# A decoder step on one core: the first pair's tokens gathered before gain and bias, a shifted first ring, and head means in fewer columns

## What is computed

```python
proj = x @ w_in                      # q, k, v of two head groups, 8 heads x 64 each
o_A = block-sparse attention over k, v (all past 256 positions here)
o_B = dilated attention, windows 128/1, 512/4, 2048/16, merged by denominators
o = concat(RMSNorm_head(o_A) * gn_moba, RMSNorm_head(o_B) * gn_win) @ w_out
x = LayerNorm(alpha * x + o)         # ln1_g, ln1_b
top-4 of 32 experts by softmax router; per expert:
  gu = x @ w_gate_up + b; act = clamped SwiGLU(gu); y = act @ w_down + b_down
x = LayerNorm(alpha * x + sum of gate * y)   # ln2_g, ln2_b
```

## Time and profile before

| | |
|---|---|
| median of 3 runs | 1183.83 us (1183.76 to 1184.81) |
| profiled execution, its own time | 1188.98 us |
| its span | 1187.1 us |
| mean granted TensorE clock | 0.986 of full |
| busy: TensorE, VectorE, ScalarE, GpSimd | 1141.0, 297.0, 175.3, 38.4 us |
| HBM read, written | 450.43 MB, 11.93 MB |

### The profile page before, as it was taken

The page is one execution under the profiler, slowest core; times in us unless marked ns, Lnnn a source line. Parts: engine busy times, 40 slices in busy tenths (PEclk is TensorE's granted clock), DMA queues, the critical chain, the costliest instruction groups (busy, mean ns, idle before and its releaser), DMA issues.

```text
span 1187.1 us, 14412 instructions
## 1 busy us (share of the span) xinstructions
PE 1141.0 (96%) x5520; PEld 469.3 (40%) x5521; DVE 297.0 (25%) x702; ACT 175.3 (15%) x381; POOL 38.4 (3%) x71
## 2 busy tenths in 40 slices
PE   8999889999999999999999999999999999999996
PEld 6877654553333333333333333333333333333332
DVE  1453756822021212121211203030303030303113
ACT  1332322211010101010202010101010111111111
POOL 0110111200000000000000000000000000000001
PEclk9999999889999999999999999999999999999998
DMA  9957749758999999999999999999999999999993
GB/s 350 320 195 255 266 176 413 305 199 344 407 427 426 428 428 427 428 428 428 428 428 428 428 428 428 428 427 428 428 428 428 428 428 427 428 428 428 413 422 123
DMA packets 83397, 454.45 MB, mean 383 GB/s; under 512 B 7146, under 2 KB 20098, under 8 KB 36130
## 3 DMA queue, kind: packets, MB, share of 16 engines
q1 hardware_dynamic: 81008, 441.49, 90.2%
q0 software_dynamic: 1728, 10.75, 2.4%
q10 hardware_dynamic: 626, 1.75, 0.4%
HBM read 450.43 MB, written 11.93 MB: 389 GB/s over the span
## 4 chain that ended last, share of the span: by engine, by line
PE 75%; DMA 18%; DVE 4%; ACT 2%; SPq 1%; issue 1%; DVEq 0%
PE bank L1055 23%; PE bank L1097 18%; DMA ring<-in_w_gate_up 16%; PE bank L1031 8%; PE bank L688 6%; PE bank L665 5%; PE bank L1122 3%; PE bank L835 2%; PE bank L691 2%; DMA ring<-in_w_down 2%; PE bank L1206 1%; PE bank L790 1%; PE bank L1138 1%; PE bank L956 1%; SPq L448 1%; ACT actT L1286 1%
## 5 line engine op out<-in xcount | busy, mean ns | idle before, releaser
L1055 PE MATMUL bank<-ring,xg 128*64 128x512 f32 x1904 | 420.6, 598 | 10.6 <-DMA ring<-in_w_gate_up 10.6
L1055 PEld LDWEIGHTS bank<-ring,xg 128*64 128x64 f32 x1904 | 133.6, 137 | 288.9 <-issue 263.6
L1097 PE MATMUL bank<-ring,actT 128*64 128x512 f32 x960 | 215.9, 597 | 3.8 <-ACT actT L1286 3.8
L1888 DVE TENSOR_TENSOR acc<-acc,bank 128x512 f32<-128x512 f32 x60 | 41.2, 687 | 493.6 <-PE bank L1122 493.6
L1097 PEld LDWEIGHTS bank<-ring,actT 128*64 128x64 f32 x960 | 66.6, 137 | 121.5 <-issue 118.7
L1429 ACT ACTIVATE sig<-gate 128x256 f32<-128x256 f32 x64 | 26.7, 417 | 528.0 <-DVE gate L1870 528.0
L1031 PE MATMUL bank<-hx,pick 128*128 128x512 f32 x180 | 90.0, 625 | 0.0
L1870 DVE TENSOR_SCALAR gate<-bank 128x256 f32<-128x256 f32 x64 | 26.9, 420 | 186.7 <-PE bank L1055 166.5
L688 PE MATMUL bank<-xT,wblk 128*128 128x288 f32 x256 | 68.4, 423 | 0.9 <-DVE xT L1517 0.9
L1122 PE MATMUL bank<-ybuf,spread 128*128 128x512 f32 x120 | 58.4, 618 | 0.0
L688 PEld LDWEIGHTS bank<-xT,wblk 128*128 128x128 f32 x256 | 49.4, 198 | 16.4 <-issue 2.4
(11 more groups left out here) (236 smaller groups left out, 724.1 us busy)
## 6 DMA issues: line engine op xcount, KB each, us to landing
ring<-in_w_gate_up SPq DMA_DIRECT2D x119, 2048.0 KB, 25.4
ring<-in_w_down SPq DMA_DIRECT2D x63, 2048.0 KB, 27.2
ring<-in_w_gate_up SPq DMA_DIRECT2D x16, 1024.0 KB, 18.7
wblk<-in_w_in SPq DMA_DIRECT2D x12, 1024.0 KB, 8.0
kring<-in_cache_k_moba SPq DMA_DIRECT2D x16, 256.0 KB, 5.0
vring<-in_cache_v_moba SPq DMA_DIRECT2D x16, 256.0 KB, 5.1
out<-in_state_k_win POOLq DMA_DIRECT2D x8, 512.0 KB, 4.8
out<-in_state_v_win POOLq DMA_DIRECT2D x8, 512.0 KB, 5.8
```

The costliest lines, as they stand in the source:

```text
L1055: ins = nc.tensor.matmul(bank[n][64 * e:64 * e + 64, :], xg[:, k, 64 * e:64 * e + 64], w[:, 2048 * e + 512 * n:2048 * e + 512 * n + 512], ...
L1097: ins = nc.tensor.matmul(bank[4 + half][64 * e:64 * e + 64, :], actT[:, j, 64 * e:64 * e + 64], w[:, at:at + 512], start=(j == 0), stop=(j ...
L1888: V.tensor_tensor(o, o, new, ALU.add).then_inc(S.added, 1)
```

## The change

1. Group A's mean squares are computed into 32 partitions a head pair (one row a head) instead of 128, so `msq` is 128x256; root and reciprocal are taken of that, and `spread_means` spreads it over the partitions by two products a pair of head pairs, in steps 20 and 21. Placing the samples of group A moves from step 20 to 24.
2. Gain and bias of the first norm are no longer applied to `hx`. The gather takes the normalised rows, and ScalarE applies gain and bias when it evacuates the turned slots, feature by partition, in eight pieces instead of two, in every pair. The sums take ALPHA x gain x hx (`scale_sums`), and ALPHA x bias as a 33rd row of the bias products.
3. The first pair is gathered as the others are, tile by tile, and turned; the samples' rows are doubled on partitions 32 to 63, so that the two halves of the features are gathered side by side in two row groups, in every pair. One full product (`keep_warm`) stands behind `place_early`.
4. The bias products of a pair are four of 128 slots instead of eight of 64.
5. In the first pair unit 6 lies in `first`, and unit u in slot u (u below 6) or u - 1; loads of the second norm's rows move. `add_biases` is split over units 4, 5 and 6.

```diff
+    ASIDE = 6
+    def slot_at_start(u):
+        return u if u < ASIDE else u - 1
...
-        load_unit(0, 0, 2)
+        sp.dma_start(ln_b[:, :], ln2_b[0:1, :].broadcast_to([128, D])).then_inc(S.ln2_in, 16)
+        load_slot(1)
...
-        load_unit(0, 0, 0, first, S.first_in)
+        load_unit(0, 0, ASIDE, first, S.first_in)
...
-        sp.wait_ge(S.hx_ready, 5)
-        sp.wait_ge(S.hx_last, 1)
-        sp.dma_start(ln_g[:, :], ln2_g[0:1, :].broadcast_to([128, D])).then_inc(S.ln2_in, 16)
-        sp.dma_start(ln_b[:, :], ln2_b[0:1, :].broadcast_to([128, D])).then_inc(S.ln2_in, 16)
+        sp.wait_ge(S.hx_raw, 2)
...
+        def free_at_start(slot):
+            if slot < ASIDE:
+                sp.wait_ge(S.unit_used, slot + 1)
+            else:
+                sp.wait_ge(S.gate_up_done, 4)
...
         load_units(0, 0, range(9, UNITS))
+        sp.wait_ge(S.sums_scaled, 6)
+        sp.dma_start(ln_g[:, :], ln2_g[0:1, :].broadcast_to([128, D])).then_inc(S.ln2_in, 16)
...
+        def spread_means(pair):
+            pe.wait_ge(S.msq_inverted, 1)
+            pe.wait_ge(S.outT_ready, pair)
+            for c in range(2):
+                j = 2 * pair + c
+                ins = nc.tensor.matmul(bank[4][:, 256 * c:256 * c + 256], heads_of[:, 128 * j:128 * j + 128], msq[:, 0, :],
+                                       start=True, stop=True)
+            ins.then_inc(S.means_spread, 1)
...
+        def gather_samples():
+            for a in range(2):
+                r = slice(NS * a, NS * a + NS)
+                nc.tensor.matmul(bank[6 + a][:, :], pick[r, 2, :], hx[r, 2, 512 * a:512 * a + 512], start=True, stop=False,
+                                 tile_position=(NS * a, 0))
+        def gather_tile(t, a):
+            return nc.tensor.matmul(bank[6 + a][:, :], pick[:, t, :], hx[:, t, 512 * a:512 * a + 512], start=False,
+                                    stop=(t == 1))
+        def gather_first():
+            pe.wait_ge(S.first_picked, 1)
+            pe.wait_ge(S.hx_low, 1)
+            gather_samples()
+            place_last()
+            pe.wait_ge(S.hx_centred, 4)
+            for a in range(2):
+                gather_tile(0, a)
+            pe.wait_ge(S.picked, 1)
+            for a in range(2):
+                pe.wait_ge(S.hx_centred, 5 + a)
+                gather_tile(1, a).then_inc(S.gathered, 1)
+        def keep_warm(n):
+            for _ in range(n):
+                nc.tensor.matmul(bank[0][:, :], ident, keep[:, 0:512], start=True, stop=True)
...
-                for e in range(2):
-                    ins = nc.tensor.matmul(bank[n][64 * e:64 * e + 64, :],
-                                           keep[r, C_SEL + SLOTS * e:C_SEL + SLOTS * (e + 1)],
-                                           bias_rows[r, :], start=True, stop=False, tile_position=(32 * n, 64 * e))
+                ins = nc.tensor.matmul(bank[n][:, :], keep[r, C_SEL:C_SEL + 2 * SLOTS], bias_rows[r, :], start=True,
+                                       stop=False, tile_position=(32 * n, 0))
...
-        gate_up(0, 0, 0, {1: turn_comb, 3: add_biases})
+        turn_slots(0, 0)
+        turn_slots(0, 1)
+        gate_up(0, 0, 0, {1: turn_comb, 4: lambda: add_biases(0), 5: lambda: add_biases(1), 6: add_sample_biases})
...
-                copy(xg[:, 4 * a:4 * a + 4, :], bank[7 - a][:, :].rearrange("p (k s) -> p k s", k=4)).then_inc(S.xg_ready, 1)
+                for k in range(4 * a, 4 * a + 4):
+                    ins = nc.scalar.activation(xg[:, k, :], bank[7 - a][:, 128 * (k % 4):128 * (k % 4) + 128], ACT.Identity,
+                                               bias=s_(c_cols + KC + k), scale=s_(c_cols + k))
+                ins.then_inc(S.xg_ready, 1)
```

More of the change, by code:

```diff
@@ L939, in place_last @@
             nc.tensor.matmul(out[:, 0:E], tri, last_tile, start=False, stop=True).then_inc(S.placed, 1)
[L941 to L955, removed]
-                ins = nc.tensor.matmul(bank[7 - k // 4][:, 128 * (k % 4):128 * (k % 4) + 128],
-                                       hx[0:rows, t, 128 * k:128 * k + 128], pick[0:rows, t, :],
-                                       start=(nth == 0 and k % 4 == 0), stop=(nth == 2 and k % 4 == 3))
-                if nth == 2 and k < 2:
-                    ins.then_inc(S.gathered, 1)
-                if nth == 2 and k % 4 == 3:
-                    ins.then_inc(S.slots_turned, 1)
+        def gather_samples():
[21 more added lines that the diff above has]
+                nc.tensor.matmul(bank[0][:, :], ident, keep[:, 0:512], start=True, stop=True)
         pe.wait_ge(wout_in[2], 16)
@@ L1004, in turn_comb, with add_biases, add_sample_biases @@
             ins.then_inc(S.comb_turned, 1)
-        def add_biases():
-            pe.wait_ge(S.combT_ready, 1)
-            pe.wait_ge(S.bdn_in, 16)
-            for j in range(4):
-                t, half = divmod(j, 2)
-                t0, rows = TILES[t]
-                if j >= 2:
-                    pe.wait_ge(S.added, j - 1)
-                nc.tensor.matmul(bank[4 + half][0:rows, :], combT[:, t0:t0 + rows],
+        def add_biases(t):
+            t0 = TILES[t][0]
+            for half in range(2):
+                if t == 0 and half == 0:
+                    pe.wait_ge(S.combT_ready, 1)
+                    pe.wait_ge(S.bdn_in, 32)
+                if t == 1:
+                    pe.wait_ge(S.added, half + 1)
+                nc.tensor.matmul(bank[4 + half][:, :], combT[:, t0:t0 + 128],
                                  bdn[:, 512 * half:512 * half + 512], start=True, stop=True).then_inc(S.spread_down, 1)
+        def add_sample_biases():
             pe.wait_ge(S.added, 3)
+            pe.wait_ge(S.sums_scaled, 2)
             for q in range(4):
                 r, c = slice(NS * q, NS * q + NS), slice(256 * q, 256 * q + 256)
-                nc.tensor.matmul(bank[4][r, 0:256], ident[0:NS, 0:NS], hx[0:NS, 2, c], start=True, stop=True,
+                nc.tensor.matmul(bank[4][r, 0:256], ident[0:NS, 0:NS], samp_x[:, c], start=True, stop=True,
                                  tile_position=(0, NS * q))
@@ L1028, in gather @@
             pe.wait_ge(S.actT_ready, turned_before)
+            gather_samples()
             for a in range(2):
-                for t, (t0, rows) in enumerate(TILES):
-                    ins = nc.tensor.matmul(bank[6 + a][:, :], pick[0:rows, t, :], hx[0:rows, t, 512 * a:512 * a + 512],
-                                           start=(t == 0), stop=(t == 2))
-                ins.then_inc(S.gathered, 1)
+                gather_tile(0, a)
+                gather_tile(1, a).then_inc(S.gathered, 1)
         def turn_slots(i, a):
@@ L1599, in scale_out, with invert_means, scale_pair @@
                             ALU.mult).then_inc(S.outT_ready, 1)
+        def invert_means():
+            dve.wait_ge(S.msq_rooted, 1)
+            V.reciprocal(msq[:, 0, :], msq[:, 0, :]).then_inc(S.msq_inverted, 1)
+        def scale_pair(pair):
+            dve.wait_ge(S.means_spread, pair + 1)
+            o = outT[:, 2 * pair:2 * pair + 2, 0:SEQ]
+            V.tensor_tensor(o, o, bank[4][:, :].rearrange("p (c q) -> p c q", c=2), ALU.mult).then_inc(S.outT_ready, 1)
         def samp_squares(g):
@@ L1696, in scales @@
             V.scalar_tensor_tensor(mv[:, 2:3], mv[:, 0:1], -1.0, mv[:, 1:2], ALU.mult, ALU.mult).then_inc(scaled, 1)
-        def gain(x, t, nth, centred, gained):
-            n = TILES[t][1]
-            for half in range(2):
-                c = slice(512 * half, 512 * half + 512)
-                dve.wait_ge(centred, 2 * nth + half + 1)
-                V.tensor_tensor(x[0:n, t, c], x[0:n, t, c], ln_g[0:n, c], ALU.mult).then_inc(gained, 1)
         def raw_sum(nth, half):
@@ L1832, in _ @@
         moments(2, 0)
-        gain(hx, ORDER[1], 1, S.hx_centred, S.hx_gained)
+        lower_half()
         choose(1)
```

178 lines of the change are left out of this document (103 added, 75 removed).

## The result

The changed kernel takes 1180.54 us (median of 17 runs, 1178.1 to 1183.78) where the kernel before, run beside it, takes 1185.14 (17 runs, 1183.76 to 1189.3): ratio 0.995, 95% interval 0.9941 to 0.996. That is 4.6 us of a forecast 17.6, outside the range of 1161 to 1175.

What follows compares the result with a forecast made beforehand. The weight stream bounds the kernel, so only work ahead of the first pair's unit 8 end counts. Terms -5.9 + 0.3 - 8.3 - 3.7 = -17.6 us gave 1166.2 us against the median, range 1161 to 1175.

Steps and rivals of the forecast that it cites:

- the anchor: End of the first pair's unit 8: each 1 us sooner there was to bring the end 1 us sooner.
- (a): Head norms of group A: a shorter reciprocal on VectorE removes two TensorE waits; net -5.9 us.
- its table: Table 0.27 MB larger, loaded while the first projections stream; +0.3 us put on the path (0 to 0.8).
- (b): From the attention sums to the first unit: the 2.63 us wait goes and the clock holds; -8.3 us.
- (c): In the first pair: no clock fall in four units (2.9 us), gather 0.8 us shorter; -3.7 us.
- (d): Shifted ring of weight units: slots 0 to 5 become free 3.5 us sooner; cost and gain 0.
- (e): Four bias products a pair in place of eight; later pairs need about 55.9 us, still hidden: 0.
- own time less median: Profiled execution's own time 1188.98 lay 5.15 us above the median 1183.83; the difference was taken as it is.
- its ends: Bounds of (b): -10 us if handoffs cost nothing and the samples hide, -1.5 if the clock falls again.
- the first rival: The clock falls all the same in the thin work after 226 us: +4 us, 1170.3 us; chance 0.30.
- the rival that some other wait takes their place: (a) is hidden because another wait replaces the two removed; only -11.7 us remains, 1172 us; chance 0.12.

Runs made afterwards that it cites:

- both33: The changed kernel with a 33rd row of zeros in samp_x, so all eight products of the samples' block have 33 rows; 1174.66 us, ratio 0.9899.
- warm1: The version best with one more full product of 128x512 ahead of the last but one placing; 1168.69 us, ratio 0.9856.
- before_c: The kernel before, unchanged, profiled once more; own time 1183.89 us.
- part_a: The kernel before with part (a) of the change alone (narrower head means, spreading products, samples placed in step 24); 1181.52 us, ratio 0.9955.
- best: The changed kernel with 33 rows throughout the samples' block, first-pair bias products behind the slot turns, units 0 to 3 awaiting four xg pieces; 1171.97 us.

## Why the prediction was wrong

The direction and the anchor were right; the sum was 14.3 us off (1180.54 against 1166.2). The difference, by its steps:

| step of the prediction | forecast | by the two profiles | off by |
|---|---|---|---|
| (a) with its table, up to the turning of tile 1 | -5.6 | 223.85 to 216.49: -7.36 | -1.8 |
| (b) from there to the first unit | -8.3 | 23.23 to 19.18: -4.05 | +4.25 |
| (c) from there to the end of unit 8 | -3.7 | 48.31 to 50.78: +2.47 | +6.2 |
| (d), (e): behind unit 8 | 0 | 891.7 to 892.45 | +0.7 |
| own time less span | same | 1.88, 2.09 | +0.2 |
| own time less median | 5.15 | 0.45 | +4.7 |

**(c) failed at "The bias products themselves ... and the samples' short ones, I leave at their length".** Four of them have 33 rows now beside four of 32, and the eight took 4.36 where they took 1.5: +2.8. "I expect no fall" failed with it: unit 7 behind them took 1.7 longer (both33 takes both back), so units 4 to 7 gave 0.8 in place of 2.9. The sum had no fall in units 0 and 1 either, and they took 1.7 longer. The gather gave 1.3 in place of 0.8. Together 2.8 + 1.7 - 0.8 - 1.3 = +2.4.

**(b) failed at the choice between its ends.** The wait of 2.63 us went and the router ran at full clock, as forecast; the clock then fell all the same at 223 us, with no gap ahead of it. That was the first rival, at a chance of 0.30 and a price of 4: the samples' gather took 1.1 more than counted, the four products 2.3 more. ScalarE's pieces, taken from a row of two copies at 0.225 each, took 2.90 / 8 = 0.36: +1.1, all of it in TensorE's wait of 2.55. By the Trainium skill (ScalarE: Activation LUTs, What ACT_TABLE_LOAD costs) scale and bias by partition add about 93 ns each to an instruction; an estimate from its figures is 0.39 us from one piece to the next. The row agrees within a tenth.

With the falls and the block removed, warm1 takes 44.0 us from the first unit (230.93) to unit 8's end (274.97), where the forecast had 44.6. In (c) the sum of the durations was thus right, and the conditions were not. In (b), from the turning of tile 1 to the first unit, warm1 takes 14.6 where the forecast comes to 14.9 (23.23 - 8.3), but by another order of work: its bias products stand in the wait for ScalarE, and unit 0 starts after four of the eight pieces. Taking the 3.3 us of the fall off the changed kernel's 19.18 (placings and gather, 222.89 to 232.02, against the same in warm1) leaves an estimate of 15.9. So here about 1.0 us was missing even at full clock, close to the 1.1 of ScalarE's pieces.

**(a) was right in its mechanism and too small.** Both waits went, as forecast, and the rival that some other wait takes their place did not come. Of the 7.36 us by the two profiles, steps 20 to 22 gave 7.44 where 5.9 was counted: the fall behind the second wait had also slowed the six transposes ahead of the projection (1.45 us at 153.16, 0.82 in the profiles where the clock was up), and a short wait of 0.27 went and the turn of 0.41 moved out too. The +0.3 put on the table was in the wrong place: the narrower mean squares cost 0.74. And 0.8 of the 7.36 is luck, for the first keys were turned at 21.62 in the profile of the prediction, where the first two projections took 11.09 us, and at 20.82 in that of the changed kernel, where they took 9.72.

**The step from profile to median failed.** "I take the difference as it is" holds only if what makes the profiled execution longer is left alone. Here the excess sat in three places: against before_c (1183.89) it was 1.55 us in the first projections, 1.7 in steps 20 to 22, which (a) removes, and 1.7 in the first pair. Another 1.3 of the 4.7 is that the median of three runs (1183.83) lay below that of seventeen (1185.14). Of -8.0 by the two profiled executions only -4.6 was left by the medians. part_a shows it alone: unit 8 ends 7.7 us sooner than in the profile of the prediction, while its times lie 5.0 below those of before by their means.

**(d) and (e) show no cost, as said.** Over 14 profiled executions the time from the end of unit 8 to the end of the span is 891.2 to 892.6 us, with the old ring (before, part_a) as with the shifted one, with eight bias products a pair as with four. Neither of the two was tried alone.

On the clock, the rule weighed in the prediction (TensorE: Matmul & The Clock Gate, HAM oscillation, in the Trainium skill) puts a fall behind idle time. In the window 223 to 224 of the changed kernel and in 271 to 273 it fell to 1.2 GHz with TensorE busy throughout, behind the router's products, the placings and the two-row biases at the one place, behind the samples' block at the other. The measurement decides: a stretch without gaps is not safe for that reason.

## What to carry to other kernels

Where small products are meant to run side by side, compare the rows and columns of neighbours as they are issued: one more row in every second product cost 3.3 us here, and a padded row took it back; a product made narrower among full ones cost 0.74 in four places. Before a profile's sum is set against a median, see whether the runs lie in groups and which of them the profile is of; the excess may sit in the very place that the change removes. And where one event sets the end, give its time in every profile: it told in one number per run, without the medians, what each edit was worth.

## What was not expected of the hardware

- Four products of 33 rows side by side take 0.64 us, four of 32 rows 0.63, and the eight alternating 4.36.
- A product of 32 columns in the place of one of 128, between full ones, put TensorE back by 0.1 to 0.3 us each time, 0.74 in four places (part_a against before_c).
- The clock fell to half at 223 and at 271 us with TensorE busy in the windows before it. One full product of 1.1 us ahead of that stretch kept it at full speed in each of the windows from 218 to 234 us, and narrowed the times from 1168.2 to 1173.7 (best, 6 runs) to 1168.4 to 1168.9 (warm1, 4 runs).
- One unchanged program gave times in two groups 4 us apart, and the place of one fall of the clock, ahead of a wait for VectorE or behind it, is 1.7 us of that.
